# Experts: the down product in three short-format passes instead of one in full format

## The chip, the cores and the metric

The kernel runs on one core of a Trainium2 chip. The core has TensorE (PE, matrix products; its weight loads are shown as PEld), VectorE (DVE), ScalarE (ACT), GpSimd (POOL) and SyncE (SP, which only issues transfers here), and 16 DMA engines. The metric is the device time in microseconds of one execution; the median of three runs is given, and one more execution was profiled.

## The reference

A layer of a streaming encoder: a mixer of two attention branches, then a mixture of experts, then a final normalisation. The change concerns the experts alone. There are 1024 tokens of 1024 values, 32 experts with a hidden width of 256, and two experts for each token. Sorted by expert, the rows of one expert are handled as a block of 128:

```python
def expert_block(args):
    xb, e = args                       # 128 rows x 1024
    return (jax.nn.silu(xb @ w_gate[e]) * (xb @ w_up[e])) @ w_down[e]
```

The third product, `... @ w_down[e]` (256 x 1024 weights), is the down product. The rows are then multiplied by their gate and added to their tokens.

## The kernel before

The program is a sequence of stages: normalisation and indexer, input projection, two attention branches, output projection with the router, the tables of the router, and then the experts (function `experts`), a stage for blocks beyond 128 rows (`overflow`) and the final normalisation (`final`). The order inside `experts` is written out by hand as five instruction streams, one for each engine, which meet in semaphores. Each runs one turn per expert. Four slots (`U = 4`) hold the weights of experts n to n+3: gate and up in `wgu`, down in `wd`.

TensorE's turn for expert n is: `gate_up(n+1)`, `hidden_T(n)`, `xpose(n+2)`, `down(n)`.

- `xpose` transposes the gathered rows `xs` (8 transposes, L1981).
- `gate_up` multiplies in the short float format fp32r in three passes. A value is split into a leading part (the value cast to fp32r, `lead`) and the rest (value minus lead, again in fp32r, `rest`); the products are lead x lead (L1993), lead x rest (L1994) and rest x lead (L1995). 8 slices of 128 rows give 24 products of 512 columns, in four parts of two slices.
- `hidden_T` transposes the two halves of the hidden rows `hm` (L2004).
- `down` multiplies `hmT` with `wd` in full f32 (L2015): four products of 512 columns, each of which the profile shows as two passes.

ScalarE (`lead`, L2049) casts the four parts of the gate/up weights to `w_lead`, which has one buffer per part, so part p of the next expert waits until TensorE is through with part p of this one (`m_gp`). It casts the transposed rows to `x_lead` (L2056), makes the sigmoid (L2063) and scales half of the result into `ye` (L2070). VectorE subtracts: `w_rest` = `wgu` - `w_lead` (L2102, in place over `wgu`, both inputs in SBUF), `x_rest` out of PSUM (L2109); it makes `hm` (L2116, L2118), copies the transposed hidden rows to `hmT` (L2125) and scales the other half of `ye` (L2137). ScalarE and VectorE work on the weights of expert n+2 in turn n, so one expert ahead of TensorE's gate product.

GpSimd turns: `gather(n+4)` copies one column of the token table (L1940) and starts an indirect DMA of the rows (L1943); `scatter(n)` copies a column of the target table (L1950), waits for both halves of `ye` (`m_ya`, `m_yd`) and starts an indirect DMA to `ys_d` (L1955).

SyncE loads the gate/up weights of an expert when the gate product that last used the slot is done (`m_gp`, L1622) and the down weights when the down product that last used it is done (`m_y`, L1628).

Of the kernel before, what the change touches and what calls it, by code (L numbers as in the profile page):

```python
# [22 lines left out]
P = 128  # L23
D = 1024
# [64 lines left out]
def hybrid_layer(nc, a, out):  # L89

    ctx = ExitStack()
    with ctx:
# [80 lines left out]
        top = keep("top", 2)  # L173
        otok = [keep(f"otok{k}", 4 * P) for k in range(2)]
# [1157 lines left out]
        with block() as blk:  # L1332
# [246 lines left out]
            def _(pool):  # L1579
# [19 lines left out]
                wts)  # L1599
# [286 lines left out]
def experts(nc, a, at, sem, block, ps, flat, con, h1, nhalf, tabs, xn2_d, ys_d, out, R_H, R_K, ss, var, rstd,  # L1886
            wts):
# [18 lines left out]
    names = ["m_tk", "m_tx", "m_xa", "m_xd", "m_gp", "m_wl", "m_wr", "m_sg", "m_h1", "m_h2", "m_th", "m_ht",  # L1906
# [6 lines left out]
    with block() as blk:  # L1913
# [17 lines left out]
        @blk.gpsimd  # L1931
        def _(pool):
            for k in range(U):
                pool.memset(xs[k][:, :], 0.0).then_inc(S["m_xz"], 1)

            def gather(n, r, u, first):
                if not first:
                    pool.wait_ge(S["m_tx"], n * 2 - 6)
                    pool.wait_ge(G[u], r * 16)
                pool.tensor_copy(tk[u][:, :], tok_i[:, bass.ds(n, 1)]).then_inc(S["m_tk"], 1)  # L1940
                pool.wait_ge(S["m_tk"], n + 1)
                pool.sem_inc(S["m_ask"], 1)
                pool.indirect_dma_start(out=xs[u][:, :], out_offset=None, in_=xn2_d,  # L1943
                                        in_offset=bass.IndirectOffsetOnAxis(ap=tk[u][:, 0:1], axis=0),
                                        bounds_check=T - 1, oob_is_err=False).then_inc(G[u], 16)

            def scatter(n, half, u, first):
                if not first:
                    pool.wait_ge(ST[u % 2], half * 16)
                pool.tensor_copy(dk[u % 2][:, :], dst_i[:, bass.ds(n, 1)]).then_inc(S["m_dk"], 1)  # L1950
                pool.wait_ge(S["m_dk"], n + 1)
                pool.wait_ge(S["m_ya"], n + 1)
                pool.wait_ge(S["m_yd"], n + 1)
                pool.sem_inc(S["m_ask"], 1)
                pool.indirect_dma_start(out=ys_d, out_offset=bass.IndirectOffsetOnAxis(ap=dk[u % 2][:, 0:1], axis=0),  # L1955
                                        in_=ye[u % 2][:, :], in_offset=None,
                                        bounds_check=2 * T - 1, oob_is_err=False).then_inc(ST[u % 2], 16)

            pool.wait_ge(S["m_xz"], U)
            for u in range(U):  # L1960
                gather(u, 0, u, True)
            for u in range(U):
                gather(u + U, 1, u, False)
                scatter(u, u // 2, u, u < 2)
            with pool.Fori(1, NE // U - 1) as r:
                for u in range(U):
                    gather(r * U + (u + U), r + 1, u, False)
                    scatter(r * U + u, r * (U // 2) + u // 2, u, False)
            for u in range(U):
                scatter(NE - U + u, (NE - U + u) // 2, u, False)  # L1970
            for k in range(2):
                pool.wait_ge(ST[k], 16 * NE // 2)
# [11 lines left out]
        def gate_up(pe, n, turn_n, u, first):  # L1984
# [4 lines left out]
            for part in range(4):  # L1989
                pe.wait_ge(S["m_wr"], n * 4 + (part + 1))  # L1990
# [28 lines left out]
        @blk.tensor  # L2019
        def _(pe):  # L2020


            def turn(n, r, u, first, up=True, ahead=True):
                if up:
                    gate_up(pe, n + 1, r + (u + 1) // U, (u + 1) % U, first)
                hidden_T(pe, n, u, first)
# [16 lines left out]
        def _(act):  # L2043
# [28 lines left out]

            def turn(n, r, u, half, first, early, ahead=True):
                if ahead:
                    for part in range(3):
                        lead(n + 2, r + (u + 2) // U, (u + 2) % U, part, False)
# [4 lines left out]
                result(n, half, u, first)  # L2081

            front(0, 0, True)
            for part in range(4):
                lead(0, 0, 0, part, True)
            front(1, 1, True)
# [3 lines left out]
            for n in range(2):  # L2090
                turn(n, 0, n, 0, True, True)
# [3 lines left out]
            turn(NE - 2, 0, 0, NE // 2 - 1, False, False, False)  # L2095
# [3 lines left out]
        def _(dve):  # L2099
# [269 lines left out]
```

## Time and profile before

| what | value |
|---|---|
| median of 3 runs (lowest to highest) | 1633.92 us (1629.78 to 1636.15) |
| profiled execution, its own time | 1635.34 us |
| its span, first to last instruction | 1633.4 us |
| mean granted TensorE clock over the span | 0.938 |
| busy over the span: PE, DVE, ACT, POOL | 1434.7, 1052.9, 650.6, 405.3 us |
| expert stage, first gate product to last scatter | about 1249 to 1581 us |

The busy times are sums over the whole span. An engine is busy while an instruction of it runs; waiting on a semaphore is not busy. The granted clock is the share of the full TensorE clock that the chip allowed. The windows of the expert stage, not these sums, say what a change in that stage meets.

### The profile page before, as it was taken

The numbers are of one execution on the slowest core, as the hardware profiler recorded it, in microseconds if no ns is written. First come the engines' busy times: TensorE is split into PE (matmuls) and PEld (weight loads), VectorE is DVE, ScalarE is ACT, GpSimd is POOL, SyncE is SP. The second block draws the span as 40 slices with busy tenths as digits, with TensorE's granted clock in tenths as the row PEclk, the third lists the DMA queues.
The fourth block names the chain that finished last, engine by engine and source line by source line (L and its number), as shares of the span: only waits on it lengthen the run. The fifth ranks groups of instructions, "written<-read, shape, count | busy, mean of one in ns | idle before, by whom it ended". The sixth has DMA issues, their size and how long they took to land. (4 is left out here: it accounts for less than half of the span.)

```text
span 1633.4 us, 21404 instructions
## 1 busy us (share of the span) xinstructions
PE 1434.7 (88%) x7182; PEld 1108.7 (68%) x7191; DVE 1052.9 (64%) x2047; ACT 650.6 (40%) x1129; POOL 405.3 (25%) x406
## 2 busy tenths in 40 slices
PE   6996899999999898988889888999945999999960
PEld 3465688889895457777667666889944777777730
DVE  4158999999922466666676665443254777777737
ACT  3157212121211236666666654021103666666622
POOL 1000322221211105454434411410002233333213
PEclk9998899999999999999999998999966999999985
DMA  7450122332231000302323204423154899999808
GB/s 195 51 87 14 58 81 87 103 97 91 73 117 42 1 0 1 72 1 66 75 60 82 66 1 161 157 87 104 65 219 182 321 357 357 356 367 376 328 31 319
DMA packets 86604, 216.82 MB, mean 133 GB/s; under 512 B 23720, under 2 KB 46792, under 8 KB 74232
## 3 DMA queue, kind: packets, MB, share of 16 engines
q1 hardware_dynamic: 76152, 194.72, 36.4%
q0 software_dynamic: 9216, 16.80, 2.8%
q10 hardware_dynamic: 1152, 4.19, 0.6%
q8 instruction: 51, 0.84, 0.2%
q14 instruction: 33, 0.27, 0.1%
HBM read 187.75 MB, written 44.70 MB: 142 GB/s over the span
## 5 line engine op out<-in xcount | busy, mean ns | idle before, releaser
L1193 DVE TENSOR_TENSOR pL<-ps,pH 128x512 fp32r<-128x512 f32 (+3 forms) x224 | 127.0, 574 | 114.4 <-ACT pH L1130 113.6
L457 DVE TENSOR_SCALAR_CACHE_REDUCE mask<-score,cand 128x272 bf16<-128x272 f32 (+6 forms) x224 | 185.5, 892 | 5.0 <-DVE cand L476 4.9
L2102 DVE TENSOR_TENSOR w_rest<-wgu,w_lead 128x1024 fp32r<-128x1024 f32 x128 | 156.0, 1223 | 45.0 <-ACT w_lead L2049 43.8
L542 PE MATMUL ps<-hHi,g_lead 128*128 128x512 f32 (+2 forms) x416 | 158.6, 381 | 16.2 <-DVE hLo L582 16.2
L543 PE MATMUL ps<-hLo,g_lead 128*128 128x512 f32 (+2 forms) x416 | 158.8, 382 | 0.0
L544 PE MATMUL ps<-hHi,g_rest 128*128 128x512 f32 (+2 forms) x416 | 158.0, 380 | 0.0
L2049 ACT CAST w_lead<-wgu 128x1024 fp32r<-128x1024 f32 x128 | 134.4, 1055 | 37.9 <-PE ps L1995 37.9
L1130 ACT CAST pH<-ps 128x512 fp32r<-128x512 f32 (+3 forms) x224 | 107.7, 488 | 71.5 <-PE ps L1078 70.5
L1993 PE MATMUL ps<-w_lead,x_lead 128*128 128x512 f32 x256 | 114.2, 446 | 6.0 <-DVE w_rest L2102 6.0
L577 POOL TENSOR_TENSOR g_rest<-g_raw,g_lead 128x2048 fp32r<-128x2048 f32 x13 | 61.7, 4745 | 227.8 <-ACT g_lead L551 227.8
L2015 PE MATMUL ps<-wd,hmT 128*128 128x512 f32 x256 | 115.3, 593 | 1.6 <-DVE hmT L2125 1.0
L1995 PE MATMUL ps<-w_lead,x_rest 128*128 128x512 f32 x256 | 101.8, 397 | 0.0
L542 PEld LDWEIGHTS ps<-hHi,g_lead 128*128 128x128 f32 x416 | 79.0, 190 | 32.9 <-issue 11.2
L1994 PE MATMUL ps<-w_rest,x_lead 128*128 128x512 f32 x256 | 100.9, 394 | 0.0
L1094 PE MATMUL ps<-pH,VS 128*128 128x512 f32 (+3 forms) x224 | 98.5, 440 | 0.2
L544 PEld LDWEIGHTS ps<-hHi,g_rest 128*128 128x128 f32 x416 | 79.1, 190 | 13.9
L543 PEld LDWEIGHTS ps<-hLo,g_lead 128*128 128x128 f32 x416 | 78.9, 190 | 14.0
L1955 POOL DMA_INDIRECT ys_d<-ye,dk x32 | 32.5, 1015 | 213.7 <-DVE ye L2137 213.7
L1095 PE MATMUL ps<-pL,VS 128*128 128x512 f32 (+3 forms) x224 | 81.4, 363 | 0.0
L563 ACT ACTIVATE stage<-ps 128x512 f32<-128x512 f32 x32 | 19.2, 598 | 151.9 <-PE ps L544 151.9
L2015 PEld LDWEIGHTS ps<-wd,hmT 128*128 128x128 f32 x256 | 46.2, 190 | 47.8 <-issue 47.8
L356 PE MATMUL ps<-hT,wslot 128*128 128x512 f32 (+2 forms) x176 | 72.1, 573 | 2.3 <-DMA wslot<-in_w_in 2.3
(332 smaller groups left out, 3453.1 us busy)
## 6 DMA issues: line engine op xcount, KB each, us to landing
wgu<-in_w_exp_gate SPq DMA_DIRECT2D x32, 1024.0 KB
wgu<-in_w_exp_up SPq DMA_DIRECT2D x32, 1024.0 KB
wd<-in_w_exp_down SPq DMA_DIRECT2D x32, 1024.0 KB
g_raw<-in_w_in SPq DMA_DIRECT2D x14, 1024.0 KB, 5.5
gates_d<-stage SPq DMA_DIRECT2D x32, 256.0 KB, 2.0
gt<-gates_d SPq DMA_DIRECT2D x32, 256.0 KB, 3.2
rel_d<-relf SPq DMA_DIRECT2D x1, 4672.0 KB
KR<-kb_d SPq DMA_DIRECT2D x16, 260.0 KB, 6.0
```

Of the source, the lines that this page charges most:

```text
L457: return dve.tensor_scalar(mask[:, OFF[i]:OFF[i + 1]], score[:, OFF[i]:OFF[i + 1]], thr, 0.0, op, ALU.add, accum_out=cnt[:, i:i + 1])
L542: pe.matmul(dst, x[0], y[0], start=(k == 0), stop=False)
L543: pe.matmul(dst, x[0], y[1], start=False, stop=False)
L544: mm = pe.matmul(dst, x[1], y[0], start=False, stop=(k == KT - 1))
L1130: act.copy(pH[n % RING][:, lo:512], bank_of(k)[:, lo:512]).then_inc(s_ld, 1)
L1193: dve.tensor_tensor(pL[n % RING][:, lo:512], bank_of(k)[:, lo:512], pH[n % RING][:, lo:512].bitcast(F32), ALU.subtract).then_inc(s_rs, 1)
L1993: pe.matmul(dst, xl[:, k, :], wl, start=(k == 0), stop=False)
L1994: pe.matmul(dst, xl[:, k, :], wr, start=False, stop=False)
L1995: mm = pe.matmul(dst, xr[:, k, :], wl, start=False, stop=(k == KT - 1))
L2015: mm = pe.matmul(ps[:, 5 + half, :], hmT[u % 2][:, k, :], wd[u][:, k, 512 * half:512 * (half + 1)], start=(k == 0), stop=(k == 1))
L2049: act.copy(w_lead[part][:, :, :, :], wgu[u][:, :, 2 * part:2 * part + 2, :]).then_inc(S["m_wl"], 1)
L2102: dve.tensor_tensor(w_rest[u][:, :, 2 * part:2 * part + 2, :], wgu[u][:, :, 2 * part:2 * part + 2, :], w_lead[part][:, :, :, :].bitcast(F3 ...
```

## The change

The down product is made like the gate/up product: three passes in fp32r over lead and rest parts. For that both of its inputs are split.

- The down weights go through four quarters (`quarters`: slice k of the hidden width, half of the 1024 columns). For each, ScalarE casts `wd` to `d_lead[q]` (`down_lead`, 128x512, one buffer per quarter, so after the previous down product, `m_y`), then GpSimd subtracts into `d_rest` in place over `wd` (`down_rest`, 128x512, waits for `m_dl`, gives `m_dr`). ScalarE does its four after `ye` of the expert before, GpSimd its four after that expert's scatter.
- The transposed hidden rows are split by ScalarE (`hT_lead`, `hidden_lead`, between its second and third part of the gate/up weights) and VectorE (`hT_rest`, in place of the copy to `hmT`). Both have a single buffer now.
- TensorE's `hidden_T(n)` moves from behind `gate_up(n+1)` to between the second and the third of its four parts. `down` has 12 products of 512 columns instead of 4 full-format ones, and waits for each quarter.

The blocks beyond 128 rows (`overflow`) keep the full format. The core of the diff:

```diff
+    quarters = [(k, slice(512 * half, 512 * (half + 1))) for half in range(2) for k in range(2)]
+    d_lead = [at(f"d_lead{q}", [P, 512], F32R, home) for q, home in
+              enumerate((R_OT, R_OT + 2048, R_H + 30720, wts["end"] + 32768))]
+    d_rest = [at(f"d_rest{u}", [P, 2, D], F32R, R_K + 24576 * u + 16384) for u in range(U)]
+    hT_lead, hT_rest = (at(f"hT_{nm}", [P, 2, P], F32R, R_H + 28672 + off) for nm, off in (("lead", 0), ("rest", 1024)))
...
+            def down_rest(n, u):
+                for q, (k, c) in enumerate(quarters):
+                    pool.wait_ge(S["m_dl"], n * 4 + (q + 1))
+                    pool.tensor_tensor(d_rest[u][:, k, c], wd[u][:, k, c], d_lead[q][:, :].bitcast(F32),
+                                       ALU.subtract).then_inc(S["m_dr"], 1)
...
             with pool.Fori(1, NE // U - 1) as r:
                 for u in range(U):
                     gather(r * U + (u + U), r + 1, u, False)
                     scatter(r * U + u, r * (U // 2) + u // 2, u, False)
+                    down_rest(r * U + (u + 1), (u + 1) % U)
...
             for part in range(4):
+                if part == 2 and between:
+                    hidden_T(pe, *between)
                 pe.wait_ge(S["m_wr"], n * 4 + (part + 1))
...
         def down(pe, n, turn_n, u, first):
-            pe.wait_ge(WD[u], turn_n * 16 + 16)
             pe.wait_ge(S["m_ht"], n + 1)
...
-            for half in range(2):
-                for k in range(2):
-                    mm = pe.matmul(ps[:, 5 + half, :], hmT[u % 2][:, k, :], wd[u][:, k, 512 * half:512 * (half + 1)],
-                                   start=(k == 0), stop=(k == 1))
+            for q, (k, c) in enumerate(quarters):
+                dst = ps[:, 5 + q // 2, :]
+                pe.wait_ge(S["m_dr"], n * 4 + (q + 1))
+                pe.matmul(dst, hT_lead[:, k, :], d_lead[q][:, :], start=(k == 0), stop=False)
+                pe.matmul(dst, hT_lead[:, k, :], d_rest[u][:, k, c], start=False, stop=False)
+                mm = pe.matmul(dst, hT_rest[:, k, :], d_lead[q][:, :], start=False, stop=(k == 1))
             mm.then_inc(S["m_y"], 1)
...
+            def down_lead(n, turn_n, u, first):
+                act.wait_ge(WD[u], turn_n * 16 + 16)
+                if not first:
+                    act.wait_ge(S["m_y"], n)
+                for q, (k, c) in enumerate(quarters):
+                    act.copy(d_lead[q][:, :], wd[u][:, k, c]).then_inc(S["m_dl"], 1)
+
+            def hidden_lead(n, first):
+                act.wait_ge(S["m_th"], n + 1)
+                if not first:
+                    act.wait_ge(S["m_y"], n)
+                act.copy(hT_lead[:, :, :], ps[:, 4, 0:2 * P].rearrange("p (k n) -> p k n", k=2)
+                         ).then_inc(S["m_hl"], 1)
+
             def turn(n, r, u, half, first, early, ahead=True):
                 if ahead:
-                    for part in range(3):
-                        lead(n + 2, r + (u + 2) // U, (u + 2) % U, part, False)
+                    lead(n + 2, r + (u + 2) // U, (u + 2) % U, 0, False)
+                    lead(n + 2, r + (u + 2) // U, (u + 2) % U, 1, False)
+                hidden_lead(n, early)
+                if ahead:
+                    lead(n + 2, r + (u + 2) // U, (u + 2) % U, 2, False)
                 back(n + 1, u + 1, False)
...
                 result(n, half, u, first)
+                down_lead(n + 1, r + (u + 1) // U, (u + 1) % U, False)
...
             def mid(n, u, first):
                 dve.wait_ge(S["m_th"], n + 1)
                 if not first:
-                    dve.wait_ge(S["m_y"], n - 1)
-                dve.tensor_copy(hmT[u % 2][:, :, :], ps[:, 4, 0:2 * P].rearrange("p (k n) -> p k n", k=2)
-                                ).then_inc(S["m_ht"], 1)
+                    dve.wait_ge(S["m_y"], n)
+                dve.wait_ge(S["m_hl"], n + 1)
+                dve.tensor_tensor(hT_rest[:, :, :], ps[:, 4, 0:2 * P].rearrange("p (k n) -> p k n", k=2),
+                                  hT_lead[:, :, :].bitcast(F32), ALU.subtract).then_inc(S["m_ht"], 1)
```

## Rows read from the trace of the kernel before

**Rows 1.** Windows: busy time of each engine, TensorE clock, DMA share and GB/s.
```profile
1400.00:1500.00 100.00, 100.00 (x420) 71.38 (x419) 77.68 (x111) 61.98 (x80) 32.59 (x40) 1.00 0.98 370
1490.00:1500.00 10.00, 10.00 (x43) 7.15 (x42) 7.88 (x12) 6.20 (x9) 3.20 (x4) 1.00 0.99 382
```

**Rows 2.** Tile view of the expert weights: SyncE issues of one load in the stage.
```profile
L1622 SPq DMA_DIRECT2D wgu<-in_w_exp_gate x23: 327/333/338, 1308.0 to 1529.0; - x23
```

**Rows 3.** Timeline of one expert turn: start, duration, engine, line [idle before <-releaser].
```profile
1392.95 0.69 ACT L2070 ACTIVATE ye<-ps,wk 128x512 f32<-128x512 f32 x1 [1.88 <-PE ps L2015]
...
1393.12 0.40 PE L1995 MATMUL ps<-w_lead,x_rest 128*128 128x512 f32 x1
...
1393.19 0.74 DVE L2137 TENSOR_SCALAR ye<-ps,wk 128x512 f32<-128x512 f32 x1
...
1394.91 1.02 POOL L1955 DMA_INDIRECT ys_d<-ye,dk  x1 [5.92 <-DVE ye L2137]
...
1395.33 1.23 DVE L2102 TENSOR_TENSOR w_rest<-wgu,w_lead 128x1024 fp32r<-128x1024 f32 x1 [1.40 <-ACT w_lead L2049]
...
1395.93 0.66 POOL L1940 COPY tk<-tok_i 128x1 int32 x1
...
1396.71 1.23 DVE L2102 TENSOR_TENSOR w_rest<-wgu,w_lead 128x1024 fp32r<-128x1024 f32 x1 [0.16 <-ACT w_lead L2049]
...
1397.44 1.41 POOL L1943 DMA_INDIRECT xs<-xn_d,tk  x1 [0.85 <-POOL tk L1940]
...
1398.16 0.39 PE L2004 MATMUL ps<-con,hm 128*128 128x128 f32 x2
...
1398.59 0.42 DVE L2125 COPY hmT<-ps 128x256 f32<-128x256 f32 x1 [0.65 <-PE ps L2004]
1398.85 0.20 POOL L1950 COPY dk<-dst_i 128x1 int32 x1
...
1398.99 1.21 DVE L2102 TENSOR_TENSOR w_rest<-wgu,w_lead 128x1024 fp32r<-128x1024 f32 x1
...
1399.28 3.60 PE L2015 MATMUL ps<-wd,hmT 128*128 128x512 f32 x8
...
1402.10 1.22 DVE L2102 TENSOR_TENSOR w_rest<-wgu,w_lead 128x1024 fp32r<-128x1024 f32 x1
```

**Rows 4.** Groups by line and shape, expert stage: count, busy us, mean ns, idle before.
```profile
L2102 DVE TENSOR_TENSOR w_rest<-wgu,w_lead 128x1024 fp32r<-128x1024 f32 x101 | 123.5, 1223 | 38.2 <-ACT w_lead L2049 37.5
L2049 ACT CAST w_lead<-wgu 128x1024 fp32r<-128x1024 f32 x102 | 107.6, 1055 | 32.7 <-PE ps L1995 32.7
...
L2056 ACT CAST x_lead<-ps 128x512 fp32r<-128x512 f32 x50 | 26.8, 588 | 9.2 <-PE ps L1981 9.2
```

**Rows 5.** Line views, expert stage: GpSimd copy and row gather, min/median/max ns.
```profile
L1940 POOL COPY tk<-tok_i x32: 187/656/708, 1238.1 to 1536.8; 128x1 int32 x24, 128x1 int32<-128x1 int32 x8
...
L1943 POOL DMA_INDIRECT xs<-xn_d,tk x32: 1015/1394/1670, 1239.2 to 1538.2; - x32
```

**Rows 6.** Line view of a GpSimd subtraction of 128x512: min/median/max ns.
```profile
L1230 POOL TENSOR_TENSOR VS<-Va,VS x8: 1268/1276/1288, 614.8 to 764.9; 128x512 fp32r<-128x512 f32 x8
```

**Rows 7.** Line view of two subtractions run on GpSimd and VectorE at once.
```profile
L582 POOL TENSOR_TENSOR hLo<-hT,hHi x4: 2572/3394/3401, 160.3 to 169.5; 128x1040 fp32r<-128x1040 f32 x4
L582 DVE TENSOR_TENSOR hLo<-hT,hHi x4: 3426/3430/3442, 160.5 to 170.6; 128x1040 fp32r<-128x1040 f32 x4
```

**Rows 8.** Groups by line and shape: a GpSimd subtraction of 128x1040 elsewhere.
```profile
L1259 POOL TENSOR_TENSOR KL<-KR,KH 128x1040 fp32r<-128x1040 f32 x8 | 19.4, 2422 | 0.6
```

**Rows 9.** Timeline where one GpSimd addition overlaps a VectorE subtraction.
```profile
1021.91 1.22 DVE L1499 TENSOR_TENSOR wb_rest<-wbr,wb_lead 128x1024 fp32r<-128x1024 f32 x1
...
1022.14 2.13 POOL L1584 TENSOR_TENSOR yT<-ytmp 128x512 f32<-128x512 f32 x1 [1.28 <-DVE ytmp L1517]
```

**Rows 10.** Windows of the attention stage: PE busy, and granted clock.
```profile
740.00:750.00 10.00, 8.50 (x64) 7.33 (x62) 7.16 (x14) 5.98 (x15) 7.28 (x9) 1.00 0.00 0
900.00:910.00 10.00, 7.02 (x38) 5.82 (x38) 5.33 (x16) 5.33 (x13) 6.03 (x7) 0.83 0.65 164
```

More of the change, by code:

```diff
@@ L173, in hybrid_layer @@
         top = keep("top", 2)
+        R_OT = small[0]
         otok = [keep(f"otok{k}", 4 * P) for k in range(2)]
@@ L1598, in hybrid_layer @@
         experts(nc, a, at, sem, block, ps, flat, con, h1, nhalf, tabs, xn2_d, ys_d, out, R_H, R_K, ss, var, rstd,
-                wts)
+                wts, R_OT)
 U = 4
@@ L1886, in experts @@
 def experts(nc, a, at, sem, block, ps, flat, con, h1, nhalf, tabs, xn2_d, ys_d, out, R_H, R_K, ss, var, rstd,
-            wts):
+            wts, R_OT):
     tok_i, dst_i, slot_w, ov_e = tabs["tok_i"], tabs["dst_i"], tabs["slot_w"], tabs["ov_e"]
@@ L1902, in experts @@
     w_lead = [at(f"w_lead{k}", [P, 2, 2, FE], F32R, wts["end"] + 16384 + 4096 * k) for k in range(4)]
+    quarters = [(k, slice(512 * half, 512 * (half + 1))) for half in range(2) for k in range(2)]
[3 more added lines that the diff above has]
+    hT_lead, hT_rest = (at(f"hT_{nm}", [P, 2, P], F32R, R_H + 28672 + off) for nm, off in (("lead", 0), ("rest", 1024)))
     w_rest = [at(f"w_rest{u}", [P, 2, KT, FE], F32R, R_K + 24576 * u) for u in range(U)]
     ident = con[:, K_ID:K_ID + P]
-    names = ["m_tk", "m_tx", "m_xa", "m_xd", "m_gp", "m_wl", "m_wr", "m_sg", "m_h1", "m_h2", "m_th", "m_ht",
+    names = ["m_tk", "m_tx", "m_xa", "m_xd", "m_gp", "m_wl", "m_wr", "m_dl", "m_dr", "m_hl", "m_sg", "m_h1", "m_h2", "m_th", "m_ht",
              "m_y", "m_ya", "m_yd", "m_st", "m_dk", "m_xz", "m_wk", "m_ask"]
@@ L1961, in _ @@
                 gather(u, 0, u, True)
+            down_rest(0, 0)
             for u in range(U):
@@ L1964, in _ @@
                 scatter(u, u // 2, u, u < 2)
+                down_rest(u + 1, (u + 1) % U)
             with pool.Fori(1, NE // U - 1) as r:
@@ L1968, in _ @@
                     scatter(r * U + u, r * (U // 2) + u // 2, u, False)
+                    down_rest(r * U + (u + 1), (u + 1) % U)
             for u in range(U):
                 scatter(NE - U + u, (NE - U + u) // 2, u, False)
+                if u < U - 1:
+                    down_rest(NE - U + u + 1, u + 1)
             for k in range(2):
@@ L1982, in xpose, with gate_up @@
                 mm.then_inc(S["m_tx"], 1)
-        def gate_up(pe, n, turn_n, u, first):
+        def gate_up(pe, n, turn_n, u, first, between=None):
             pe.wait_ge(S["m_xd"], n * 2 + 2)
@@ L2024, in turn @@
                 if up:
-                    gate_up(pe, n + 1, r + (u + 1) // U, (u + 1) % U, first)
-                hidden_T(pe, n, u, first)
+                    gate_up(pe, n + 1, r + (u + 1) // U, (u + 1) % U, first, (n, u, first))
+                else:
+                    hidden_T(pe, n, u, first)
                 if ahead:
@@ L2085, in _ @@
                 lead(0, 0, 0, part, True)
+            down_lead(0, 0, 0, True)
             front(1, 1, True)
@@ L2090, in _ @@
             for n in range(2):
-                turn(n, 0, n, 0, True, True)
+                turn(n, 0, n, 0, True, n == 0)
             with act.Fori(0, (NE - 4) // 4) as r:
@@ L2094, in _ @@
                     turn(r * 4 + (u + 2), r + (u + 2) // U, (u + 2) % U, r * 2 + (1 + u // 2), False, False)
-            turn(NE - 2, 0, 0, NE // 2 - 1, False, False, False)
+            turn(NE - 2, NE // U - 1, U - 2, NE // 2 - 1, False, False, False)
+            hidden_lead(NE - 1, False)
             result(NE - 1, NE // 2 - 1, 1, False)
```

## The prediction, made before the change was run

> **What bounds the kernel now.** I first took the page's slices, to see where the changed code runs: the expert stage fills the last quarter of the span up to the final normalisation, and nothing outside it is edited. Then the windows of that stage [rows 1]: TensorE is busy in all 100 of 100 us at a granted clock of 1.00, VectorE in 78, ScalarE in 62, GpSimd in 33, and the DMA engines have a busy share of 0.98 at 370 GB/s. So TensorE sets the pace and the transfers stand close behind. The length of one expert's turn comes from the weight loads, which SyncE issues once per turn: 22 intervals in 1529.0 - 1308.0 us [rows 2], 10.05 us each.
>
> The timeline splits that turn [rows 3]. From the third gate/up product (1393.12) to the first transpose of the hidden rows (1398.16) lie 22 products in 5.04 us, 0.229 us each, so 24 take 5.50. From there to the first down product (1399.28) the ten transposes take 1.12. The down product has what is left, 10.05 - 5.50 - 1.12 = 3.43 us for its eight passes, 0.43 each. The reader is to see that no idle time stands before a TensorE row, while GpSimd stands idle 5.9 us before its scatter, and also that GpSimd's copy of 128x1 elements takes 0.66 us when VectorE's `w_rest` lies over it: it starts at 1395.93 and ends at 1396.59, and that `w_rest` runs from 1395.33 to 1396.56. Alone this copy takes 0.19 [rows 5].
>
> **TensorE's part.** Removed: 8 passes of 0.43. Added: 12 products in the short format, 12 x 0.229 = 2.75 us. Its own work falls by 0.68 us to 9.37 per turn; over 31 turns that would be 21 us. The transposes of the hidden rows move from the end of the gate product to between its second and third part: the same two instructions, no other queue involved. What that gives is time for the hidden rows, which now need two steps (`hT_lead` on ScalarE, then `hT_rest` on VectorE, about 0.4 each, for one `hmT` copy of 0.42 [rows 3]); half a gate product, 2.75 us, covers them, so they cost TensorE nothing. At the old place they would have had only the eight transposes, about 0.9 us.
>
> **ScalarE's part.** Added per turn: four casts of 128x512 and one of 128x256. The nearest rows are `x_lead`, 0.588 for the same size out of PSUM, and `w_lead`, 1.055 for twice the size out of SBUF [rows 4]; halves give 0.53, I take 0.55: 2.2 us, and 0.38 for the small one. ScalarE goes from 6.2 to about 8.8 us per turn, below 9.37. In the order of its queue the four casts stand between `ye` and the next `w_lead`, so with the end of the down product at 0, `ye` takes until 0.7, the casts until 2.9, and the first two `w_lead` end at about 4.0 and 5.0 (before the change 2.3 and 3.7 after it [rows 3]). Who waits for them is VectorE's `w_rest`, which is a whole turn ahead of its use, so this lateness alone costs nothing. The four casts for expert 0 stand in front of a wait for TensorE's first gate product, 5.5 us long, and are hidden there.
>
> **VectorE's part.** One 128x256 subtraction out of PSUM takes the place of one copy of the same size: nothing. Its 7.8 us per turn stay. But it gets a wait, below.
>
> **GpSimd's part, which decides.** Each turn it gathers (copy 0.19, gap 0.85, indirect DMA 1.02) and scatters (copy 0.20, gap of 0.98 after `ye`, indirect DMA 1.02): 4.26 us with nothing in the way [rows 3, 5], 5.12 as it stands now, since `w_rest` lies over the copy and over the gather. Added: four subtractions of 128x512 with both inputs in SBUF. The same form takes 1.276 us [rows 6], 5.1 per turn. Its own work is then 4.26 + 5.1 = 9.4 us per turn, already as much as TensorE's, and all of it in series: `down_rest(n+1)` stands behind `scatter(n)`, the next gather and scatter stand behind `down_rest(n+1)`.
>
> To this comes that these subtractions and VectorE's `w_rest` (also two inputs in SBUF) do not run side by side. Where both engines subtracted 128x1040 at once, GpSimd took 3.39 us and VectorE 3.43 [rows 7], while GpSimd alone needs 2.42 for that [rows 8] and VectorE 1.22 for 1024 [rows 4]: they take turns, one instruction each, and each GpSimd instruction grows by 0.97. One addition of 128x512 that met a VectorE subtraction took 2.13 [rows 9]; it ended 1.14 after the other one had ended. That is 0.85 more than alone. The Trainium skill has this as a rule (SBUF — State Buffer, section Who interferes with whom): a VectorE instruction with two SBUF inputs and a GpSimd instruction that reads SBUF exclude each other for the whole instruction. Taken to the letter it would add the full 1.22 of a `w_rest` for each one met, and the turn worked out below would be 13.5 instead of 12.5.
>
> How many are met? With the end of the down product at 0: GpSimd comes late out of its gather, scatters from about 2.8 to 3.8, and its four subtractions begin there; unhindered they would last until 8.9. The `w_rest` of parts 0, 1 and 2 ask at about 4.0, 5.1 (behind the first) and 8, when the hidden rows and the third `w_lead` are through: all three fall among the subtractions. The fourth falls on the gather or its copy. Three meetings at 0.85 to 0.97 are 2.7 us, the fourth I take at 0.4, half of the 0.86 by which two of them lengthen copy and gather now. GpSimd's turn: 9.4 + 2.7 + 0.4 = 12.5 us. It stands against TensorE 9.4, ScalarE 8.8, VectorE 7.8 + 3 x 1.15 = 11.3. The fourth quarter of `d_rest` is then ready at 3.8 + 5.1 + 2.7 = 11.6, TensorE needs 0.69 for its three products, and the next down product ends at about 12.4, which closes the circle. TensorE, ready for the down product at 6.7, stands idle some 3 us in each turn.
>
> **The sum.** 12.5 - 10.05 = 2.45 us per turn. It holds for 29 of the 32 turns; in the last ones there is no `w_rest` any more, and they come out as before within 1 us. 29 x 2.45 = +71 us. The profiled execution took 1635.3 us, its span 1633.4; the runs shown have a median of 1633.9, 1.4 less, which I leave aside: 1635 + 71 = 1706. Lower end: only two meetings at 0.85 and the gather free, 9.4 + 1.7 = 11.1 per turn, +1.05 x 29 = +30, 1665. Upper end: all four at 0.97, 9.4 + 3.9 = 13.3, +3.2 x 29 = +94, 1730.
>
> **Rivals.**
>
> A. The exclusion doesn't reach these instructions, or `w_rest` slips into GpSimd's gaps (it has 4.3 us of gather and scatter). For it: part of the gather and scatter is a gap in which GpSimd reads nothing. Against it: rows 7 and 9, and that ScalarE's leads come just when the subtractions run. It decides if all meetings together stay below 0.65 us per turn. Then the turn is TensorE's 9.4 and the kernel faster by up to 0.68 x 31 = 21, 1614. The transfers would take part of that: a turn moves 370 x 10.05 = 3.72 MB, and the fastest 10 us of the stage show 382 GB/s [rows 1], so a turn of 9.7 at least, 10 us gained, 1625. Chance 0.06.
>
> B. As A, but the transfers hold the turn where it is, at 10.05: 370 GB/s at a share of 0.98 is their end. Result 1635, no change. Against it: 382 in one window. Chance 0.05. The Trainium skill (DMA: Bandwidth & Descriptors, section Specifications) gives about 358 GB/s of HBM for a core; by that the 3.72 MB would take 10.4 us and this rival would hold already now. The rows with 370 to 382 GB/s do not bear that out.
>
> C. TensorE's clock falls, because it is now idle in a quarter of the time. In the attention stage a window with 8.5 of 10 us busy has 1.00, one with 7.0 has 0.83 [rows 10]. At 0.83 TensorE's 9.4 become 11.3, still below GpSimd's 12.5, and only the pacing of the `w_lead` suffers, some 0.5 us per turn, 1720, inside the range. If it stayed at the lower level (1.2 of 2.4 GHz) throughout, the turn would be 18.7 and the time 1886; over a fifth of the turns, 1742. Chance of ending above 1730 this way 0.06.
>
> The forecast itself (GpSimd's turn of 11.1 to 13.3) has 0.83. Faster and slower begin 0.5% away, 8 us, about what a measurement of this kernel can tell from no change: faster 0.06 (A), same 0.05 (B), slower 0.89 (the forecast and C). The range of 1665 to 1730 leaves out A, B and the bad end of C, 0.17.
>
> **What would show it.** In the windows of the expert stage GpSimd should go from 33 to above 85 in 100 us, TensorE from 100 to about 75 to 80; the weight loads should be issued every 12.5 us; `d_rest` should last 2.1 to 2.3 us in most cases and about 1.28 where nothing is met; `w_rest` should rise above 1.22 in the mean; TensorE's idle time should stand before the down product with `d_rest` as the releaser. The down product's rows should have a spacing of 0.229. `hT_rest` should not be a releaser of any length. DMA should fall to about 300 GB/s. Wrong it would be if `d_rest` stays at 1.28 with `w_rest` over it (then A), if TensorE waits for `w_rest` or for ScalarE rather than for `d_rest` (then I have placed the queue wrongly), or if the clock is well below 0.9.

## The result and the profile after

The changed kernel takes 1790.32 us (median of 4 runs, 1787.98 to 1792.80) against 1631.85 for the kernel before in the same comparison (4 runs, 1626.76 to 1636.15): a ratio of 1.097, 95% interval 1.0948 to 1.0996. It is slower, as forecast, but by 158 us where 71 were forecast, and outside the range of 1665 to 1730. The profiled execution took 1789.0 us, its span 1787.2.

The loss is all in the expert turns. Tile view of the changed kernel, SyncE's register step with each load of the gate weights, once per turn from turn to turn:

```profile
L1623 SPq MOVE wgu<-in_w_exp_gate x24: 29/29/29, 1264.2 to 1611.7; - x24
```

23 intervals in 1611.7 - 1264.2 give 15.11 us per turn, where [rows 2] gave 10.05. 5.06 more for some 30 turns are 152 us, and the two profiled executions differ by 1789.0 - 1635.3 = 153.7. Every turn below is read from this row of its kernel, so that they compare.

Windows of the changed kernel in the order of [rows 1]: 100 us of the stage, then a stretch of one turn in which TensorE works on gate/up products, then that turn's down product.

```profile
1400.00:1500.00 100.00, 75.46 (x294) 61.19 (x295) 76.12 (x76) 50.13 (x80) 55.56 (x50) 0.81 0.64 232
1482.80:1488.40 5.60, 5.60 (x27) 4.63 (x26) 2.34 (x3) 5.30 (x9) 3.53 (x3) 1.00 0.62 215
1493.50:1498.70 5.20, 5.19 (x12) 4.10 (x13) 4.23 (x7) 0.00 (x0) 1.18 (x2) 0.51 0.55 221
```

TensorE went from 100 to 75 and the transfers from 370 to 232 GB/s, but no engine took its place as the busy one: VectorE 76, GpSimd 56, ScalarE 50. A turn bound by one engine's work would show that engine near 100. This one is a loop of waits. The clock's mean of 0.81 is no even slowness either: 1.00 while the gate/up products run, 0.51 in the down product.

Groups of the page (count, busy us, mean ns, idle before and its releaser), then the line views of the two subtractions (min/median/max ns), then the waits of 1320 to 1680 us (total, times, longest):

```profile
L2143 DVE TENSOR_TENSOR w_rest<-wgu,w_lead 128x1024 fp32r<-128x1024 f32 x128 | 266.9, 2106 | 86.4 <-ACT w_lead L2070 86.2
L2034 PE MATMUL ps<-d_lead,hT_lead 128*128 128x512 f32 x128 | 77.9, 609 | 116.5 <-DVE hT_rest L2167 112.6
L1968 POOL TENSOR_TENSOR d_rest<-wd,d_lead 128x512 fp32r<-128x512 f32 x128 | 161.3, 1297 | 4.8 <-ACT d_lead L2099 4.1
```

```profile
L2143 DVE TENSOR_TENSOR w_rest<-wgu,w_lead x128: 1206/1218/5661, 1243.6 to 1711.5; 128x1024 fp32r<-128x1024 f32 x128
L1968 POOL TENSOR_TENSOR d_rest<-wd,d_lead x128: 1254/1288/2362, 1247.0 to 1729.1; 128x512 fp32r<-128x512 f32 x128
```

```profile
POOL ys_d L1961 <- DVE ye L2179: 126.5, 23, 6.0
PE ps L2034 <- DVE hT_rest L2167: 92.8, 24, 3.9
DVE w_rest L2143 <- ACT w_lead L2070: 71.5, 24, 3.0
```

The reader is to see who pays. GpSimd's `d_rest` hardly ever grows: its median, 1.288 us, is that of one which meets nothing [rows 6]. VectorE's `w_rest` has kept its median and has a tail up to 5.66, more than four times its length in [rows 4]. And TensorE waits, up to 3.9 us per turn, not for `d_rest` but for `hT_rest`, a subtraction of 0.41 us. The timeline of one turn tells why:

```profile
1482.58 0.39 PE L2036 MATMUL ps<-d_lead,hT_rest 128*128 128x512 f32 x1
...
1483.12 0.75 DVE L2179 TENSOR_SCALAR ye<-ps,wk 128x512 f32<-128x512 f32 x1 [0.29 <-PE ps L2036]
...
1483.69 2.17 ACT L2099 CAST d_lead<-wd 128x512 fp32r<-128x512 f32 x4
...
1484.85 1.02 POOL L1961 DMA_INDIRECT ys_d<-ye,dk  x1 [5.09 <-DVE ye L2179]
...
1485.56 0.39 PE L2023 MATMUL ps<-con,hm 128*128 128x128 f32 x2
...
1485.89 5.01 POOL L1968 TENSOR_TENSOR d_rest<-wd,d_lead 128x512 fp32r<-128x512 f32 x4
...
1486.84 6.28 DVE L2143 TENSOR_TENSOR w_rest<-wgu,w_lead 128x1024 fp32r<-128x1024 f32 x2 [2.97 <-ACT w_lead L2070]
...
1487.66 0.36 ACT L2105 CAST hT_lead<-ps 128x256 fp32r<-128x256 f32 x1
...
1490.85 1.17 POOL L1946 COPY tk<-tok_i 128x1 int32 x1
...
1493.04 0.41 DVE L2167 TENSOR_TENSOR hT_rest<-ps,hT_lead 128x256 fp32r<-128x256 f32 x1
...
1493.51 0.79 PE L2034 MATMUL ps<-d_lead,hT_lead 128*128 128x512 f32 x1 [3.91 <-DVE hT_rest L2167]
1494.10 0.63 PE L2035 MATMUL ps<-d_rest,hT_lead 128*128 128x512 f32 x1
...
1498.91 0.75 DVE L2179 TENSOR_SCALAR ye<-ps,wk 128x512 f32<-128x512 f32 x1 [1.15 <-PE ps L2036]
```

GpSimd's four subtractions run back to back in 5.01 us, 1.25 each. VectorE asks with its first `w_rest` at 1486.84, while the first of them runs, and its two take 6.28 us together instead of 2.44: it gets in only behind the last one, at about 1490.9. Below, this keeping out is called the lock. The hidden rows, transposed at 1485.56 to 1485.95, are cast by 1488.0 (ScalarE's `hT_lead`); but `hT_rest` stands behind both `w_rest` in VectorE's queue and comes at 1493.04. (In all 22 turns between 1300 and 1635 us the four subtractions stay together, and the first `w_rest` takes 5.12 to 5.16 us.) Then 12 products at a spacing of 0.43 us, and `ye`, which lets the next scatter go, and behind that the next four subtractions. The loop is: `ye`, scatter, four subtractions, two `w_rest`, `hT_rest`, down product. In TensorE's terms this turn is 10.7 us from the end of one down product (1482.81) to the start of the next (1493.51), where gate/up and transposes have 6.8 and 3.91 are idle, and 5.2 us for the down product itself.

### The profile page after: what moved, and what is told of

It is laid out like the page before. It is cut to its first block and busy times, and to the rows that moved or that the text cites. A ratio compares the mean times of both kernels' runs of the same rounds, so it can differ in the third digit from the quotient of the medians.

```text
span 1787.2 us, 22161 instructions
## 1 busy us (share of the span) xinstructions
PE 1473.5 (82%) x7310; PEld 1172.8 (66%) x7319; DVE 1163.7 (65%) x2047; ACT 713.1 (40%) x1289; POOL 584.9 (33%) x534
## 5 line engine op out<-in xcount | busy, mean ns | idle before, releaser
L2143 DVE TENSOR_TENSOR w_rest<-wgu,w_lead 128x1024 fp32r<-128x1024 f32 x128 | 266.9, 2106 | 86.4 <-ACT w_lead L2070 86.2
L2034 PE MATMUL ps<-d_lead,hT_lead 128*128 128x512 f32 x128 | 77.9, 609 | 116.5 <-DVE hT_rest L2167 112.6
L1968 POOL TENSOR_TENSOR d_rest<-wd,d_lead 128x512 fp32r<-128x512 f32 x128 | 161.3, 1297 | 4.8 <-ACT d_lead L2099 4.1
L2034 PEld LDWEIGHTS ps<-d_lead,hT_lead 128*128 128x128 f32 x128 | 37.6, 294 | 131.7 <-DVE hT_rest L2167 97.9
L2012 PE MATMUL ps<-w_lead,x_lead 128*128 128x512 f32 x256 | 104.9, 410 | 6.0 <-DVE w_rest L2143 6.0
L2091 ACT ACTIVATE ye<-ps,wk 128x512 f32<-128x512 f32 x32 | 22.0, 689 | 217.1 <-PE ps L2036 217.1
L1214 POOL TENSOR_TENSOR otok<-otmp,rec 128x256 f32<-128x256 f32 x32 | 19.6, 613 | 214.8 <-DVE otmp L1201 214.8
```

The costliest lines, as they stand in the source:

```text
L1968: pool.tensor_tensor(d_rest[u][:, k, c], wd[u][:, k, c], d_lead[q][:, :].bitcast(F32), ALU.subtract).then_inc(S["m_dr"], 1)
L2012: pe.matmul(dst, xl[:, k, :], wl, start=(k == 0), stop=False)
L2034: pe.matmul(dst, hT_lead[:, k, :], d_lead[q][:, :], start=(k == 0), stop=False)
L2143: dve.tensor_tensor(w_rest[u][:, :, 2 * part:2 * part + 2, :], wgu[u][:, :, 2 * part:2 * part + 2, :], w_lead[part][:, :, :, :].bitcast(F3 ...
```

## The experiments

Each kernel is the changed one with an edit of its own; *ye on ScalarE* builds on *d_rest on VectorE*, *both* on *ye on ScalarE*, and *rows of 520* edits the kernel before. The table has the time against the kernel before on the same chip, and the turn from the 24 register steps as above (before: 1267.8 to 1499.0, 10.05; after: 15.11).

| | median us | ratio [95%] | turn, us |
|---|---|---|---|
| write only | 1619.94 | 0.9933 [0.991, 0.9956] | 9.62 |
| drained | 1719.01 | 1.0534 [1.0494, 1.0574] | 12.86 |
| hT_rest first | 1754.40 | 1.0751 [1.0719, 1.0782] | 13.94 |
| TensorE filled | 1770.39 | 1.0848 [1.0816, 1.0881] | 14.47 |
| d_rest on VectorE | 1629.04 | 0.9981 [0.9963, 0.9999] | 9.94 |
| one wide | 1790.62 | 1.0967 [1.0929, 1.1004] | 15.10 |
| one input | 1679.10 | 1.0284 [1.0249, 1.0318] | 11.53 |
| half in short format | 1628.52 | 0.9972 [0.9959, 0.9985] | 9.89 |
| rows of 520 (one run) | 1622.65 (before: 1631.42) | | 10.05 |
| ye on ScalarE | 1626.78 | 0.9964 [0.9951, 0.9978] | 9.65 |
| both | 1619.92 | 0.9926 [0.9911, 0.9942] | 9.65 |
| subtractions ahead of scatter | 1732.34 | 1.0619 [1.0594, 1.0645] | 13.44 |

**Write only.** Is it the reading that holds VectorE off, or GpSimd's occupation? GpSimd writes zeros in place of the four rests, so this kernel leaves them out of the down product. They stand behind an addition of one column (`tick`) that carries the wait.

```diff
-                    pool.tensor_tensor(d_rest[u][:, k, c], wd[u][:, k, c], d_lead[q][:, :].bitcast(F32),
-                                       ALU.subtract).then_inc(S["m_dr"], 1)
+                pool.tensor_tensor(tick[:, 0:1], tick[:, 1:2], tick[:, 2:3], ALU.add).then_inc(S["m_tick"], 1)
...
+                    pool.memset(d_rest[u][:, k, c].bitcast(F32), 0.0).then_inc(S["m_dr"], 1)
```

> GpSimd's four subtractions are replaced by four plain writes of zeros of the same 128x512 pieces, behind one add of a single column that carries the wait; the rest pass over the down weights therefore adds nothing to the result. Theory 1 (VectorE is locked out of its second SBUF input while GpSimd subtracts, and hT_rest is queued behind the two w_rest that are held up): no w_rest longer than 1.3 us, TensorE finds hT_rest ready, turn 9.5 to 9.9 us, kernel about 1620 to 1632. Theory 2 (the three-pass down product or its single buffers are at fault whatever GpSimd does): the turn stays above 12 us, kernel above 1690.

1619.94 us, a turn of 9.62. The window and the tile view of `w_rest`:

```profile
1400.00:1500.00 100.00, 100.00 (x477) 82.52 (x476) 79.67 (x116) 84.04 (x135) 73.88 (x92) 1.00 0.98 381
```

```profile
L2146 DVE TENSOR_TENSOR w_rest<-wgu,w_lead x124: 1207/1218/1249, 1254.4 to 1546.0; 128x1024 fp32r<-128x1024 f32 x124
```

`w_rest`'s tail is gone (1.249 at most), TensorE is busy in 100 of 100 us at full clock and nothing is left of the 158 us. So the whole loss comes from GpSimd's subtractions, by their reads or by their length, and what follows from them. GpSimd is freer here as well (a zero quarter takes 0.5 us), which the next kernel excludes as the cause. The turn stands at 9.6 and not at TensorE's own 9.37, at a DMA share of 0.98 and 381 GB/s: about the floor that rival A gave to the transfers (9.7 at 382). That the transfers hold it there is likely, but no run tests it.

**Drained.** Each subtraction also waits for the completion of the one before it on GpSimd itself. The same instructions and a little more time for GpSimd.

```diff
                     pool.wait_ge(S["m_dl"], n * 4 + (q + 1))
+                    if q:
+                        pool.wait_ge(S["m_dr"], n * 4 + q)
```

> Each of GpSimd's four subtractions now waits until the one before has finished, which puts a small gap between them; nothing else is changed. Theory 1a (the lock goes to VectorE as soon as GpSimd has no next reading instruction waiting at its engine): w_rest falls from 5.1 us to about 2.3, the d_rest of later quarters rise to about 2.2, the turn goes from 15.1 to 12.5 to 13.5, as the forecast had it, kernel 1705 to 1740. Theory 1b (GpSimd wins the pair every time, gap or not): turn unchanged at 15.1, kernel 1790.

1719.01, a turn of 12.86: 71 us less, by one wait added. The timeline of the two, and the waits of 1320 to 1600 us:

```profile
1448.38 4.77 DVE L2145 TENSOR_TENSOR w_rest<-wgu,w_lead 128x1024 fp32r<-128x1024 f32 x2 [2.25 <-ACT w_lead L2072]
...
1448.55 7.97 POOL L1970 TENSOR_TENSOR d_rest<-wd,d_lead 128x512 fp32r<-128x512 f32 x4
```

```profile
PE ps L2036 <- DVE hT_rest L2169: 46.5, 22, 2.5
```

Two `w_rest` take 4.77 instead of 6.28 and four `d_rest` 7.97 instead of 5.01: now they take turns. `d_rest`'s median is 2.07 and GpSimd is busy in 82 of 100 us. This is the picture that I had forecast for the change itself (2.1 to 2.3, above 85, a turn of 12.5), and its time is in the forecast's range. So the exclusion was priced rightly under a condition that the change does not meet. It also shows that GpSimd's load is not the cause: it is busy for 10.8 us of each turn (mean of 11 turns) where it was 8.7 (mean of 23), and the kernel takes 71 us less.

**hT_rest first.** Only the order in VectorE's queue is changed: `hT_rest` in front of the first three `w_rest`.

```diff
+                mid(n, u, first)
                 if ahead:
-                    for part in range(2):
+                    for part in range(3):
                         rest(n + 2, (u + 2) % U, part)
-                mid(n, u, first)
-                if ahead:
-                    rest(n + 2, (u + 2) % U, 2)
```

> On VectorE hT_rest stands ahead of the first two w_rest instead of behind them. Theory 1 says that TensorE then no longer waits 3.9 us for hT_rest, but that VectorE's chain, ye, four subtractions of GpSimd, then all four w_rest and the work on x and the hidden rows, takes over: turn 14.0 to 14.6, kernel 1755 to 1775. If only the place of hT_rest in the queue were at fault (rival), the turn would fall to 10 us or less and the kernel to 1640.

1754.40, just under the expected 1755 to 1775. Timeline:

```profile
1442.09 5.04 POOL L1968 TENSOR_TENSOR d_rest<-wd,d_lead 128x512 fp32r<-128x512 f32 x4
...
1443.71 0.42 DVE L2167 TENSOR_TENSOR hT_rest<-ps,hT_lead 128x256 fp32r<-128x256 f32 x1 [3.65 <-ACT hT_lead L2105]
...
1444.11 6.38 DVE L2143 TENSOR_TENSOR w_rest<-wgu,w_lead 128x1024 fp32r<-128x1024 f32 x3
```

`hT_rest` runs in 0.42 in the middle of GpSimd's subtractions: with one input in PSUM it is not kept out. The three `w_rest` then lose their time, and `x_rest`, next in the queue, makes TensorE wait (up to 3.7 us). The place in the queue decides who is late, and changing it recovers 36 us; the lock, and a clock of 0.85 over 1400 to 1500 us, are still there.

**TensorE filled.** 14 products more into a bank that nothing reads, in front of each down product, to keep the clock up.

```diff
+                    xf = x_lead[(u + 1) % 2]
+                    for _ in range(14):
+                        pe.matmul(ps[:, 7, :], xf[:, 0, :], xf[:, 0:4, :], start=True, stop=True)
                 down(pe, n, r, u, first)
```

> 14 extra products of 512 columns into an unused PSUM bank stand between the transposes of x and the down product, in TensorE's idle time of 3.9 us. The clock theory (idle time lets the granted clock fall to half, so that the down product takes 5.2 us instead of 2.75): with TensorE busy the clock stays at 1.00, the down product takes 2.8, the turn falls by 0.9 to 2.4 us, kernel 1715 to 1765. If the clock costs nothing on the path: 1790 or more, since 3.2 us of products are added.

1770.39, 5 us above what I expected. Timeline of TensorE, and of the following `ye` in the turn before:

```profile
1434.99 3.45 PE L2052 MATMUL ps<-x_lead 128*128 128x512 f32 x14
1440.23 0.50 PE L2034 MATMUL ps<-d_lead,hT_lead 128*128 128x512 f32 x1 [1.78 <-DVE hT_rest L2170]
...
1443.10 0.40 PE L2012 MATMUL ps<-w_lead,x_lead 128*128 128x512 f32 x1
```

```profile
1428.60 1.22 DVE L2146 TENSOR_TENSOR w_rest<-wgu,w_lead 128x1024 fp32r<-128x1024 f32 x1
...
1429.74 0.74 DVE L2182 TENSOR_SCALAR ye<-ps,wk 128x512 f32<-128x512 f32 x1
```

At a granted clock of 1.00 the down product takes 2.87 us (1443.10 - 1440.23). In the changed kernel long and shorter ones alternate from turn to turn: 5.2 in the turn above and 4.23 in the one before it, which begins so and ends at the 1482.81 shown above:

```profile
1478.58 0.80 PE L2034 MATMUL ps<-d_lead,hT_lead 128*128 128x512 f32 x1 [3.77 <-DVE hT_rest L2167]
```

Their mean, 4.7, is 1.8 us above 2.87, and the turn keeps only 0.64 of it. VectorE gives 1.0 back: the down product now ends (1428.44) before VectorE has started its fourth `w_rest`, so `ye` starts 1.30 after that end instead of 0.31, and the scatter and its followers with it. The clock is worth 20 us of the 158 as the kernel stands, not the 1.8 x 30 = 54 that its rows suggest.

**d_rest on VectorE.** VectorE makes `d_rest` after its `ye`; GpSimd only gathers and scatters.

```diff
-                    down_rest(r * U + (u + 1), (u + 1) % U)        (GpSimd, behind scatter)
...
                 result(n, half, u, first)
+                down_rest(n + 1, (u + 1) % U)                      (VectorE)
```

> VectorE makes d_rest itself, four subtractions of 128x512 right after its half of ye, where it has 3 us of idle time; GpSimd only gathers and scatters, as before the change. Theory 1 (the lock between GpSimd's and VectorE's reads is the loss, not the work on d_rest): the four take 2.4 us, nothing is held up, VectorE is the fullest engine with 7.8 + 2.4 = 10.2 us, turn 10.1 to 10.6, kernel 1633 to 1650. A rival by which the split of the down weights is too much on any engine: turn above 12, kernel above 1690.

1629.04, 4 us below the expected band: 0.68 us per quarter, and VectorE is full.

```profile
1400.00:1500.00 100.00, 96.93 (x463) 79.72 (x462) 99.65 (x151) 81.93 (x131) 29.05 (x41) 1.00 0.96 373
```

The same arithmetic, with no subtraction on GpSimd, gives back everything. ScalarE's share and the three passes themselves cost nothing.

**One wide.** Was it the size? In the input stage pieces of 128x1040 took turns [rows 7]; here they are 128x512. The first two quarters become one subtraction of 128x1024.

```diff
+                pool.wait_ge(S["m_dl"], n * 4 + 2)
+                pool.tensor_tensor(d_rest[u][:, :, 0:512], wd[u][:, :, 0:512], d_lead01[:, :, :].bitcast(F32),
+                                   ALU.subtract).then_inc(S["m_dr"], 2)
+                for q, (k, c) in list(enumerate(quarters))[2:]:
```

> GpSimd's first two subtractions of 128x512 are made one of 128x1024, the other two stay. In the stage before, where the two engines took turns, GpSimd's instructions had 1040 columns. If the size decides who gets the read port next: VectorE's w_rest gets in behind the wide one and falls to about 2.5 us, kernel 1730 to 1760. If only a gap between GpSimd's instructions lets VectorE in: the three subtractions still run back to back in 4.9 us, w_rest 5 us, kernel 1780 to 1795.

```profile
1440.78 2.41 POOL L1968 TENSOR_TENSOR d_rest<-wd,d_lead 128x1024 fp32r<-128x1024 f32 x1
...
1441.76 6.11 DVE L2147 TENSOR_TENSOR w_rest<-wgu,w_lead 128x1024 fp32r<-128x1024 f32 x2 [2.99 <-ACT w_lead L2074]
```

1790.62, no difference. VectorE does not get in behind the wide one either. Size is out.

**One input.** GpSimd copies `d_lead` alone, one input in SBUF, and leaves out the rests; `tick` carries the wait as in *write only*.

```diff
+                    pool.tensor_copy(d_rest[u][:, k, c], d_lead[q][:, :].bitcast(F32)).then_inc(S["m_dr"], 1)
```

> GpSimd's subtractions are replaced by copies of d_lead of the same 128x512 size, so with one input in SBUF instead of two (the rest pass then works with wrong weights; the rest values themselves are left out), behind one small add that carries the wait. If one input is enough to hold VectorE off: four copies of about 0.6 us back to back, a w_rest that meets them is longer by up to 2.4 us, turn 10 to 11, kernel 1632 to 1665. If only instructions with two inputs in SBUF exclude each other: every w_rest 1.22, turn 9.5 to 9.9 as with the plain writes, kernel 1618 to 1628.

1679.10, above both expectations. Timeline of GpSimd and VectorE:

```profile
1442.95 4.02 DVE L2146 TENSOR_TENSOR w_rest<-wgu,w_lead 128x1024 fp32r<-128x1024 f32 x2 [1.91 <-ACT w_lead L2073]
1443.05 1.17 POOL L1969 TENSOR_TENSOR tick<-tick 128x1 f32<-128x1 f32 x1
...
1444.17 3.26 POOL L1971 CAST d_rest<-d_lead 128x512 fp32r<-128x512 f32 x4
```

An addition of one column takes 1.17 us because a `w_rest` is under way, and the copies (0.6 us each by themselves) then put the second `w_rest` off; it comes in before the fourth, which takes 1.59. So one read input is enough. A shorter run of reads goes with a shorter turn here (11.53 against 15.11), but length is not the whole price, as the next kernel shows.

**Half in short format.** Columns 0 to 511 in three passes, 512 to 1023 in the full format as before: two subtractions per turn, ahead of the scatter, and a full copy of the hidden rows beside the two parts.

```diff
+            for k in range(2):
+                pe.matmul(ps[:, 6, :], hT_full[:, k, :], wd[u][:, k, 512:1024], start=(k == 0), stop=(k == 1))
```

> Only columns 0 to 511 of the down product go in three short-format passes, columns 512 to 1023 stay in full format and are multiplied first; ScalarE makes two casts of the weights instead of four and one more copy of the hidden rows; GpSimd makes two subtractions, and makes them ahead of its scatter, when VectorE waits for ScalarE anyway. TensorE's own turn is then 9.37 + 0.34 = 9.7 us, no longer than what the transfers need. Theory 1: d_rest runs from 1.3 to 3.9 us after the down product's end, holds back the first w_rest by at most 1 us and TensorE not at all; turn 9.7 to 9.9, kernel 1620 to 1628, faster than before by 0.3 to 0.7%. If GpSimd's subtractions cost TensorE time wherever they stand: 1640 or more.

1628.52, just above the expected band. `w_rest` still rises to 2.23 us at most, and TensorE stays busy in 100 of 100: two subtractions in a row (2.54 us), where they now stand, fit into VectorE's slack. Against rival B it shows that a turn below 10.05 is to be had.

**Rows of 520.** The other way round, in the input stage of the kernel before: GpSimd's pieces are halved, two subtractions on one wait.

```diff
+                    for c in range(2):
+                        r = slice(L // 2 * c, L // 2 * (c + 1))
+                        mm = pool.tensor_tensor(hLo[:, k, r], hT[:, k, r], hHi[:, k, r].bitcast(F32), ALU.subtract)
+                    mm.then_inc(s_hp, 1)
```

> The kernel before, and in it only the place where GpSimd and VectorE took turns (the subtraction of the leading part of the input rows, 128x1040, GpSimd 3.39 us and VectorE 3.43 each): GpSimd's four instructions are halved to eight of 128x520, of which the second of each pair has no wait of its own. If an instruction of at most about 1024 columns keeps the read port for the next one: GpSimd's eight run in 10 us, 1.25 each, and one of VectorE's takes more than 8 us. If the engines take turns whenever both wait: VectorE's four take about 2.3 us each, with one piece of 1.15 us in between. Whole kernel 1633 either way.

Line views, which answer to [rows 7]:

```profile
L590 POOL TENSOR_TENSOR hLo<-hT,hHi x8: 1302/1879/2297, 156.0 to 168.9; 128x520 fp32r<-128x520 f32 x8
```

```profile
L582 DVE TENSOR_TENSOR hLo<-hT,hHi x4: 2329/2329/2335, 156.2 to 163.0; 128x1040 fp32r<-128x1040 f32 x4
```

Here the engines go on taking turns, with small pieces and no wait between the two of a pair: VectorE's subtraction is 2.33 = its own 1.2 and one half piece, where it was 3.43. VectorE comes through sooner: its four end 9.1 us after they begin, where it was 13.5. The one run of the kernel is 9 us faster (1622.65 against 1631.42), which I had not expected, with the expert turn as it was. The four subtractions account for 4.4 of the 9; where the rest comes from is not shown.

**ye on ScalarE.** *d_rest on VectorE*, with the second half of `ye` moved to ScalarE, and the hidden rows split after the first weight part.

```diff
+                act.activation(ye[u % 2][:, 512:1024], ps[:, 6, :], ACT.Copy,
+                               scale=wk[u % 2][:, 0:1]).then_inc(S["m_yd"], 1)
...
-                result(n, half, u, first)
```

> On top of the kernel in which VectorE makes d_rest (turn 9.99 us, VectorE busy 99.65 of 100): ScalarE makes both halves of ye, and hT_lead and hT_rest stand behind the first part of the gate/up weights instead of the second. VectorE's work falls from 10.0 to 9.3 us per turn, ScalarE's rises from 8.2 to about 8.9. If VectorE's work was the bound there, the turn now ends at what the transfers allow, 9.6 to 9.8 us, kernel 1615 to 1625. If a wait from ScalarE to VectorE takes its place (the later ye and d_lead), the turn stays at 10.0 and the kernel at 1629 or above.

1626.78, 2 us above the expected band. VectorE has 96 and ScalarE 89 of 100 us, and the transfers a share of 0.98 at 377 GB/s.

**Both.** That and the halved pieces of *rows of 520*.

> The kernel with VectorE making d_rest and ScalarE making ye, and with it the halved pieces of GpSimd in the earlier subtraction of the input rows, where the one look at the halved pieces took 1622.7 against 1631.4. If that gain of about 4 us in the earlier stage is real (VectorE's four subtractions end 4.4 us earlier), both add up: 1618 to 1624, faster than before by 0.5 to 0.8%. If it was chance: 1625 to 1628, as without it.

1619.92 us (6 runs, 1617.69 to 1620.88), 0.7% below the kernel before and the version to keep. Both parts show: the turn of 9.65 in the stage, and 7 us ahead of it (its first register step is at 1257.2, that of *ye on ScalarE* at 1264.1), 4.4 of them in the halved pieces.

```profile
1400.00:1500.00 100.00, 97.92 (x473) 80.16 (x472) 95.03 (x142) 88.38 (x143) 42.19 (x42) 1.00 0.98 378
```

**Subtractions ahead of the scatter.** The changed kernel with only GpSimd's order changed.

```diff
-                    scatter(r * U + u, r * (U // 2) + u // 2, u, False)
                     down_rest(r * U + (u + 1), (u + 1) % U)
+                    scatter(r * U + u, r * (U // 2) + u // 2, u, False)
```

> The changed kernel, with GpSimd's four subtractions ahead of its scatter instead of behind it. Theory 1 sums the chain from one down product's end to the next: ye and scatter no longer stand in it (2.9 us until the first subtraction become 1.4), the subtractions end at 6.4 instead of 7.9, both w_rest at 8.7, hT_rest at 9.1. With the down product at the lower clock (5.2 us) the turn is 14.2, at the full clock (2.75) 11.9: kernel 1690 to 1755. If GpSimd's total work were the bound, its order would change nothing: 1790.

```profile
1443.08 7.30 DVE L2143 TENSOR_TENSOR w_rest<-wgu,w_lead 128x1024 fp32r<-128x1024 f32 x2 [1.20 <-ACT w_lead L2070]
...
1443.17 4.98 POOL L1968 TENSOR_TENSOR d_rest<-wd,d_lead 128x512 fp32r<-128x512 f32 x4
...
1450.31 0.41 DVE L2167 TENSOR_TENSOR hT_rest<-ps,hT_lead 128x256 fp32r<-128x256 f32 x1
```

1732.34, a turn of 13.44. In this turn the lock is as long as ever (7.30 for two `w_rest`). But that holds for every other turn only. The turn before it:

```profile
1429.96 7.06 POOL L1968 TENSOR_TENSOR d_rest<-wd,d_lead 128x512 fp32r<-128x512 f32 x4 [3.42 <-ACT d_lead L2099]
...
1432.41 3.46 DVE L2143 TENSOR_TENSOR w_rest<-wgu,w_lead 128x1024 fp32r<-128x1024 f32 x2 [2.97 <-ACT w_lead L2070]
...
1435.80 0.41 DVE L2167 TENSOR_TENSOR hT_rest<-ps,hT_lead 128x256 fp32r<-128x256 f32 x1
```

Here `w_rest` asks just as GpSimd's second subtraction ends (2.45 us after the first began, two of them take 2.5). It gets in at once, and from there the engines take turns: 7.06 for the four subtractions, 3.46 for two `w_rest`. In the turns between, `w_rest` asks 0.1 us before the first subtraction and is kept out by all four (6.2 us for the one). The two kinds alternate through the stage. So both behaviours occur in the same stage, at the same size and with the same instructions. The kernel is 58 us faster than the changed one. That the scatter is out of the loop and that every other turn escapes the long lock both go that way; how the 58 divide was not measured.

## Why the prediction missed the size

**Right.** That the exclusion of a reading GpSimd and a two-input VectorE decides the case, and makes it slower: *write only* and *d_rest on VectorE* take one side of it away, and nothing is left of the loss. The single prices too: four casts 2.17 (2.2 forecast), a subtraction 1.288 (1.276), a spacing of 0.23 for the down products at full clock, the moved transposes free, ScalarE far from being the bound (50 in 100). The Trainium skill's rule (SBUF — State Buffer, section Who interferes with whom), by which a GpSimd instruction that only writes is not excluded, agrees with 1.249 at most for `w_rest` in *write only*. Near rival A's floor for the transfers, 9.7, is where the fastest kernels without the lock end up, 9.62 to 9.65.

**The step that failed** is "they take turns, one instruction each, and each GpSimd instruction grows by 0.97". From [rows 7, 9] I took that a run of subtractions is cut open by VectorE after each one. In the changed kernel it is not: GpSimd keeps its four together, grows by nothing, and VectorE bears the whole delay. With that "three meetings at 0.85 to 0.97" became one lock of 4 us, and the pacing engine was no longer GpSimd, which stood idle 5 to 6 us per turn before its scatter where I had it busy above 85. *Drained* supplies what makes them take turns, and comes out at 12.86 per turn against my 12.5. A sign that I had named misled as well: `d_rest` staying at 1.28 with `w_rest` over it was to mean rival A, a faster kernel. It did stay at 1.288, and it meant the longer lock.

**The second, in the same place:** "`hT_rest` should not be a releaser of any length". I had put VectorE at 11.3 us of work and let `w_rest` be "a whole turn ahead of its use, so this lateness alone costs nothing". Its own lateness does cost nothing; what stands behind it in the same queue is needed at once. The instruction that gets stuck was not the one to look at, but the next one. With the turns of *drained* it is still a releaser, of up to 2.5 us.

**Mis-sized: the clock.** Rival C had its mean right (0.83 forecast, 0.81 in the window above and 0.83 over 1280 to 1680 us) and the place wrong: I spread it over the turn, as some 0.5 us, and it fell on the down product, which is in the loop: 4.7 us in the mean instead of 2.87. By itself it is worth 0.64 per turn, 20 us. Together: the turn of *drained* to that of the changed kernel is 2.25 us, the main part of the 2.6 that I missed.

**Open.** When subtractions of GpSimd stay together and when they take turns with VectorE. *One wide* speaks against the size, *rows of 520* shows that no wait between two is needed in the input stage, and *ahead of the scatter* that neither the place behind the scatter nor the stage decides it: there the two kinds of turn differ in the moment at which `w_rest` asks. The moment alone is no rule that these traces bear out. In the input stage VectorE asked 0.25 us after GpSimd's first one began and got in behind it; in the expert stage it asked 0.95 us after that, still during the first, and was kept out by all four. No run varied the moment by itself.

## What to carry to other kernels

When an operation is added on GpSimd that reads SBUF, price it from both sides, once as taking turns and once as a lock of the whole run of such instructions, put on VectorE, and then look at what stands behind the locked instruction in VectorE's queue. That turns are taken in one place of a kernel doesn't say so for another, nor even for the next turn. A wait on its own completion between GpSimd's instructions (71 us here), or the order around the run (58 us), may be worth more than the work. If VectorE has the room, the same subtraction is cheaper there than on GpSimd: 0.68 us per quarter against 1.29 with a lock.

## What the runs showed of the hardware

- Behind GpSimd's reading instructions, back to back, a two-input VectorE instruction that takes 1.22 us by itself took up to 5.66, and 6.25 in *TensorE filled*, which is four subtractions and its own time; one with an input in PSUM ran beside them in 0.42. With a wait on completion between them they alternated (`w_rest` 1.905, `d_rest` 2.07 in the median), and without one they did so in every other turn of *subtractions ahead of the scatter*.
- One SBUF input on GpSimd is enough (`w_rest` up to 2.98), and one column waits as well: 1.17 us for an addition of 128x1 under a `w_rest`.
- In the changed kernel TensorE's idle time of 3.8 to 3.9 us before each down product was followed by the lower level for 6 to 12 products (spacing 0.43 instead of 0.23; granted clock 0.51 over 5.2 us), and by 1.00 in the next gate/up products, turn after turn.
- The transfers of one core held 376 to 381 GB/s over 100 us in *write only*, *half in short format*, *ye on ScalarE* and *both*.
